# The first feed-forward's first sixteen up-projection units, computed in two token halves with a PSUM bank each

## What is computed

```python
def _sq_relu_mlp(x, w1, w2):
    return jnp.square(jax.nn.relu(x @ w1)) @ w2

    x = _layer_norm(DEEPNORM_ALPHA * x + h, ln1_g[layer], ln1_b[layer])
    x = _layer_norm(DEEPNORM_ALPHA * x + _sq_relu_mlp(x, mlp_w1[layer], mlp_w2[layer]), ln2_g[layer], ln2_b[layer])
```

## Time and profile before

| | us |
|---|---|
| median of 3 runs | 3371.52 (3370.47 to 3371.78) |
| the profiled execution, its own time | 3368.43 |
| its span, first to last instruction | 3366.6 |
| TensorE (PE) busy in it | 3186.2 (95%) |
| VectorE (DVE) busy | 1863.8 (55%) |
| ScalarE (ACT) busy | 1162.7 (35%) |
| mean DMA rate | 79 GB/s |
| mean granted TensorE clock | 0.978 of full |

### The profile page before, as it was taken

How to read it: one execution, slowest core, us unless ns; L and a number is a source line. 1 busy time by engine, 2 the same in 40 slices (tenths; PEclk the granted TensorE clock), 3 DMA queues, 4 the chain that set the end, 5 groups by cost and what they waited for, 6 DMA issues and landing times.

```text
span 3366.6 us, 41464 instructions
## 1 busy us (share of the span) xinstructions
PE 3186.2 (95%) x16984; PEld 2479.4 (74%) x16984; DVE 1863.8 (55%) x2802; ACT 1162.7 (35%) x1805; POOL 158.1 (5%) x129
## 2 busy tenths in 40 slices
PE   9899789999899988999899999999999999999999
PEld 6678668887677766888577577788887757778887
DVE  3854554243677755333476755564647675466463
ACT  4433233231433334222343323332335333333232
POOL 1221010000000010000100000100010000010000
PEclk9999889999999989999999999999999999999999
DMA  4110012222211111222211122223232112222322
GB/s 173 63 52 19 2 63 100 88 100 88 71 63 63 63 50 64 99 90 98 96 63 63 38 100 88 88 87 107 83 99 89 63 38 94 94 88 87 107 82 81
DMA packets 41560, 264.84 MB, mean 79 GB/s; under 512 B 4600, under 2 KB 4984, under 8 KB 13980
## 3 DMA queue, kind: packets, MB, share of 16 engines
q1 hardware_dynamic: 41364, 262.18, 22.8%
q10 hardware_dynamic: 8, 0.01, 0.0%
HBM read 260.07 MB, written 3.42 MB: 78 GB/s over the span
## 4 chain that ended last, share of the span: by engine, by line
PE 75%; DVE 9%; ACT 3%; issue 2%; DVEq 0%; ACTq 0%; POOL 0%; POOLq 0%
PE psum L339 22%; PE psum L340 22%; PE psum L341 22%; DVE w_lo L320 1%; PE psum L921 1%; PE psum L912 1%; PE psum L765 1%; ACT tiles L942 1%; DVE tiles L1653 1%; PE psum L1849 1%; PE psum L1851 1%; PE psum L1850 1%; DVE tiles L967 1%; ACT xT L796 1%; PE psum L1761 1%
## 5 line engine op out<-in xcount | busy, mean ns | idle before, releaser
L339 PE MATMUL psum<-hi,w_hi 128*128 128x512 f32 x3672 | 1479.5, 403 | 47.8 <-DVE lo L777 26.6
L340 PE MATMUL psum<-lo,w_hi 128*128 128x512 f32 x3672 | 1458.3, 397 | 0.0
L341 PE MATMUL psum<-hi,w_lo 128*128 128x512 f32 x3672 | 1457.1, 397 | 0.0
L339 PEld LDWEIGHTS psum<-hi,w_hi 128*128 128x128 f32 x3672 | 693.9, 189 | 232.5 <-issue 30.1
L320 DVE TENSOR_TENSOR w_lo<-ring,w_hi 128x1024 fp32r<-128x1024 f32 (+1 forms) x495 | 601.5, 1215 | 424.5 <-ACT w_hi L312 424.4
L312 ACT ACTIVATE w_hi<-ring 128x1024 fp32r<-128x1024 f32 (+1 forms) x495 | 505.3, 1021 | 942.0 <-PE psum L341 880.2
L340 PEld LDWEIGHTS psum<-lo,w_hi 128*128 128x128 f32 x3672 | 694.4, 189 | 171.1 <-issue 6.8
L341 PEld LDWEIGHTS psum<-hi,w_lo 128*128 128x128 f32 x3672 | 693.5, 189 | 170.4
L730 DVE SCALAR_TENSOR_TENSOR xT<-xT,psum 128x512 f32<-128x512 f32 x96 | 65.9, 687 | 239.0 <-PE psum L341 239.0
L942 ACT ACTIVATE tiles<-tiles,small 128x256 f32<-128x256 f32 (+3 forms) x176 | 95.0, 541 | 145.4 <-DVE small L967 144.6
L1529 DVE TENSOR_TENSOR tiles<-tiles 128x512 f32<-128x512 f32 x64 | 44.3, 693 | 180.5 <-ACT tiles L1521 180.5
(11 more groups left out here) (251 smaller groups left out, 2557.8 us busy)
## 6 DMA issues: line engine op xcount, KB each, us to landing
ring<-in_weights SPq DMA_DIRECT2D x211, 1024.0 KB, 4.8
ring<-in_weights SPq DMA_DIRECT2D x28, 704.0 KB, 4.0
ring<-in_weights SPq DMA_DIRECT2D x4, 896.0 KB, 4.5
ring<-in_weights SPq DMA_DIRECT2D x3, 832.0 KB, 4.2
xT<-in_x SPq DMA_DIRECT2D x8, 256.0 KB, 5.6
tiles<-bias_repeated SPq DMA_DIRECT2D x8, 256.0 KB, 7.2
out<-xT SPq DMA_DIRECT2D x8, 256.0 KB, 2.9
held<-in_const SPq DMA_DIRECT2D x1, 1344.0 KB, 7.7
```

The costliest lines, as they stand in the source:

```text
L339: pe.matmul(out, hi, rhs.hi(first + at), start=(at == 0), stop=False)
L340: pe.matmul(out, hi, rhs.lo(first + at), start=False, stop=False)
L341: last = pe.matmul(out, lo, rhs.hi(first + at), start=False, stop=(at == end))
```

## The change

Only the first up (the first 16 units of the first layer's feed-forward) uses a new function `squared_relu_halves` with `half_products` in place of `squared_relu` with `Core.product`. The other three ups stay. For each unit, TensorE first computes tokens 0 to 255 of all 8 blocks into bank 2(t % 4), then tokens 256 to 511 of all 8 blocks into bank 2(t % 4) + 1: 48 matmuls of 256 columns instead of 24 of 512. Each half ends in a signal, and ScalarE takes relu of each half by itself. The waits on `rhs_ready` in tick 0 stand in the first half only. A bank pair is reused after 4 units. `w.left` gives the count of relus that the down projection waits for.

```diff
+def half_products(k, pe, banks, n, rhs, rhs_ready, done):
+    pe.wait_ge(k.lo_ready, n + 1)
+    for g in range(2):
+        cols = slice(g * T // 2, (g + 1) * T // 2)
+        for i in range(UNITS[n]):
+            if rhs_ready is not None and g == 0:
+                pe.wait_ge(rhs_ready, i + 1)
+            w = slice(i * P, (i + 1) * P)
+            hi, lo = k.w_hi[:, n % AHEAD, w], k.w_lo[:, n % AHEAD, w]
+            pe.matmul(banks[g][:, 0:T // 2], hi, rhs.hi(i)[:, cols], start=(i == 0), stop=False)
+            pe.matmul(banks[g][:, 0:T // 2], hi, rhs.lo(i)[:, cols], start=False, stop=False)
+            last = pe.matmul(banks[g][:, 0:T // 2], lo, rhs.hi(i)[:, cols], start=False, stop=(i == UNITS[n] - 1))
+        last.then_inc(k.unit_used if g else done, 1)
+
+def squared_relu_halves(k, first, rhs, out, rhs_ready):
...
+    def tensor(pe, t):
+        if t >= 4:
+            pe.wait_ge(relu_done, 2 * (t - 3))
+        banks = [k.bank(2 * (t % 4)), k.bank(2 * (t % 4) + 1)]
+        half_products(k, pe, banks, first + t, rhs, rhs_ready if t == 0 else None, half_done)
+
+    def scalar(act, t):
+        for g in range(2):
+            if g == 0:
+                act.wait_ge(half_done, t + 1)
+            else:
+                act.wait_ge(k.unit_used, first + t + 1)
+            if t >= 2:
+                act.wait_ge(out_lo, t - 1)
+            act.activation(buf[t % 2][:, cols[g]], k.bank(2 * (t % 4) + g)[:, 0:T // 2], ACT.Relu).then_inc(relu_done, 1)
+        k.split_hi(act, first + t + AHEAD)
+        act.wait_ge(squared, t + 1)
+        act.activation(out.hi(t), buf[t % 2], ACT.Copy).then_inc(out_hi, 1)
+
+    def vector(dve, t):
+        dve.wait_ge(relu_done, 2 * t + 2)
...
@@
-        up, n = mlp_up(k, n, xs, hidden, ln.out_lo)
+        up = squared_relu_halves(k, n, xs, hidden, ln.out_lo)
+        n += MLP_HALF
@@ mlp_down
-                            free=lambda pe, t: pe.wait_ge(up.relu_done, MLP_HALF - 7 + t))
+                            free=lambda pe, t: pe.wait_ge(up.relu_done, up.left(t)))
```

More of the change, by code:

```diff
@@ L1534, in squared_relu @@
     w = Work(MLP_HALF, tensor, scalar, vector, end=first + MLP_HALF)
-    w.relu_done, w.out_lo = relu_done, out_lo
+    w.relu_done, w.out_lo, w.left = relu_done, out_lo, lambda t: MLP_HALF - 7 + t
+    return w
+def half_products(k, pe, banks, n, rhs, rhs_ready, done):
[11 more added lines that the diff above has]
+        last.then_inc(k.unit_used if g else done, 1)
@@ new lines, in squared_relu_halves @@
+def squared_relu_halves(k, first, rhs, out, rhs_ready):
+    half_done, relu_done, squared, out_hi, out_lo = (k.sem() for _ in range(5))
+    buf = [k.tile(0), k.tile(1)]
+    cols = [slice(0, T // 2), slice(T // 2, T)]
+    def tensor(pe, t):
[17 more added lines that the diff above has]
+        dve.wait_ge(relu_done, 2 * t + 2)
+        dve.tensor_tensor(buf[t % 2], buf[t % 2], buf[t % 2], ALU.mult).then_inc(squared, 1)
+        k.split_lo(dve, first + t + AHEAD)
+        dve.wait_ge(out_hi, t + 1)
+        dve.tensor_tensor(out.lo(t), buf[t % 2], out.hi(t).bitcast(F32), ALU.subtract).then_inc(out_lo, 1)
+    w = Work(MLP_HALF, tensor, scalar, vector, end=first + MLP_HALF)
+    w.relu_done, w.out_lo, w.left = relu_done, out_lo, lambda t: 2 * MLP_HALF - 7 + t
```

## The result

| | before | after |
|---|---|---|
| median of 20 runs each, us | 3370.40 (3365.60 to 3373.05) | 3375.62 (3370.70 to 3379.83) |
| ratio after / before | | 1.0017, 95% interval 1.0011 to 1.0023 |
| span of the profiled execution, us | 3366.6 | 3368.9 |

The change costs 5.2 us by the medians (3.7 to 7.8 by the interval). That is slower, and less than the 0.2% that the prediction called measurable; it took 20 runs of each to see it. The forecast was +11.1 us. The time of 3375.6 lies in the stated range, almost on the rival of growing excess (3375.2). That the two nearly coincide is partly chance: the rival puts 3.7 us on the earlier median of 3371.5, and measured are 5.2 us on 3370.4.

A forecast was written before the change was run, and what follows sets the result against it. TensorE's own pace was taken to bound the stage. Units 1 to 15 (7.2), unit 0 (2.7) and the clock (1.2) summed to +11.1 us, forecast 3382.6 us; range 3371 to 3392.

The forecast's parts named there:

- rival of growing excess: First up: excess grows with columns, 116.7 ns per half matmul, only unit 0 pays; 3375.2 us, chance 0.22.
- TensorE's pace bounds the stage, ScalarE has room: First up: TensorE sets the pace; ScalarE waits up to 3.5 us a unit, so its added 0.17 us costs nothing.
- The pace of a 256-column matmul: First up: 126.7 ns, from 106.7 of columns plus a per-instruction 20.0; bounds 112 and 135 ns; chance 0.50.
- The term of 15 x 0.48 = 7.2 us: Units 1 to 15: 48 matmuls of 126.7 ns (6.08 us) replace 5.60 us a unit; bounds -3.4 to +13.2 us.
- The rule of the Trainium skill: Matmul pace is columns over 2.4 GHz plus about 2.5 ns: 109 ns at 256 columns, total 3369.5 us.
- Unit 0 outside the shadow: Unit 0: 27 half matmuls left after the layer norm's last lo, 3.4 us plus 0.1 where 0.80 was; +2.7 us.
- The clock: Unit 0: clock may rise as before (0 us) or only after 486 (+2.3 us); middle taken, +1.2 us.
- No cost elsewhere: VectorE, bank reuse, weight splits, down projection, DMA and SyncE add nothing.
- The sum: Whole kernel: 7.2 + 2.7 + 1.2 = +11.1 us on TensorE, giving 3382.6 us.
- The chance of 0.69 for a loss over 0.2%: Whole kernel: slower by more than 6.7 us, from 0.50 + 0.13 + 0.07, less a little.
- the 0.29: Whole kernel: chance that the time stays within 0.2%, 6.7 us, of no change.
- Load-bound at 187 ns: Units 1 to 15 and 0: weight loads do not overlap, 8.98 us a unit, +56 us, 3427 us; chance 0.07.

The follow-up runs named there:

- the filled shadow: Changed kernel plus three unread 256-column matmuls behind each of unit 0's first seven blocks; 3371.97 us against 3370.86 for the kernel before, ratio 1.0004.
- The run with exchanged loops: Changed kernel, but unit 0 computes both token halves of a block before waiting for the next lo tile; 3371.01 us against 3370.72 for the kernel before.
- two variants with halved units: Changed kernel with unit 0 at full width (3369.62 us), or with unit 0's halves done block by block (3371.01 us); kernel before 3370.72 us.
- the quarters run: Changed kernel with units 1 to 15 in four token quarters, 128-column matmuls, unit 0 still in halves; one run, 3445.83 us against 3370.86 for the kernel before.

## Why the prediction was right, and where it was wrong

- **TensorE's pace bounds the stage, ScalarE has room.** Right. A half relu took 386 ns (forecast 384 from the attention's evictions), and the second of each unit still waited for TensorE. I had said over 3 us of waiting a unit; it is 0.94 and 2.41, 3.35 together.
- **The pace of a 256-column matmul.** Wrong, and this is nearly the whole miss. I took 126.7 ns, the excess of 20.0 ns per instruction; it was 116.7, an excess of 10.0. The step that failed is the carrying over from f32 to fp32r: f32's excess of some 7 ns is the same at two widths, but fp32r's is of another size, which the rows already said, and at 256 columns it is half of that at 512. Why, the runs do not show. The term of 15 x 0.48 = 7.2 us is zero. It was mis-sized inside its own bounds (-3.4 to +13.2). The range held the time because it reached down to 3371, to f32's own pace, and not because the sum was right. The rival "growing excess" named what happened, with 22%.
- **The rule of the Trainium skill** (TensorE: Matmul & The Clock Gate, section "Back-to-back issue gap"). By it a matmul would take 109 ns, with a small gain. The trace has 116.7 at 256 columns and 233.3 at 512: neither width agrees. Leaning on it would have erred to the other side, by 8 ns a matmul.
- **Unit 0 outside the shadow.** Right in mechanism and size. The forecast was 2.7 us at 126.7 ns, which is 2.45 at the true pace; the filled shadow measured 2.45. The run with exchanged loops shows the cause. With the late clock, unit 1's first matmul came 5.03 us after the last wait (486.84 to 491.87), inside the 3.5 to 5.8 that were named.
- **The clock.** Right in mechanism, low in size: 1.2 us taken as the middle of 0 and 2.3; the filled shadow measured 1.78. I had no ground for the middle. The filled shadow shows that the lesser work under the norm kept the clock down.
- **No cost elsewhere** (banks, splits, down, DMA). Right: 85.00 us in two variants with halved units, and through the rest of this feed-forward the delay stays what it was, 5.03 us in the weight splits at 592.92 (before 587.89) and 839.32 (834.29).
- **The sum.** Unit 0 with the clock was forecast at 3.9 us and is 4.2; the medians say 5.2, whose interval (3.7 to 7.8) holds 4.2. With 0 in place of 7.2 the prediction would have been 3375.4. The chance of 0.69 for a loss over 0.2% rested on the wrong term; the loss was 0.17%, which fell to the 0.29.
- **Load-bound at 187 ns.** Rightly held unlikely. The record of a load lasts 192 ns in the quarters run too, but loads overlap: the matmuls start 111.6 ns apart, each with its own load.

## What to carry to other kernels

On an engine that takes its work in the program's order, ask of every loop that you cut or exchange where its waits come to stand: work behind the last of a row of waits no longer lies under the work that is waited for. Here one such unit was all of the loss, and 15 others were free; putting more independent work between the same waits won some 7 us over two layers instead. And before carrying an overhead from one kind of instruction to another, see whether its size agrees where both keep the array busy equally long (here 213 ns of columns, for which f32 took 220 and fp32r 233); if it does not, keep both laws, per instruction and per column, at equal weight.

## What the runs showed of the hardware

- fp32r matmuls of 512, 384 and 256 columns start 233.3, about 176.7 and 116.7 ns apart at 2.4 GHz; 128 columns take 111.6, so 128-column fp32r matmuls cost nearly as much as those of 256. At 1.2 GHz the starts are 0.21 apart at 256 columns: there it is the columns' own time (256 / 1.2 GHz = 213 ns).
- The same words read as bf16 with a step of 4 bytes ran at 226.7 and 115.0 ns, with weight-load records of 98 ns in place of 187; I had expected 216 or no change.
- With half the columns under the layer norm, the clock stayed at 1.2 GHz 8 us longer (until 490.8 instead of 482.4). Useless matmuls in the gaps brought it up again by 482, and that was worth 1.78 us.
- A full-width unit and its weight loads overlap: in 88.00 us PE was busy 87.97 and PEld 70.71.
